# Five landing pads instead of four for the expert weights, and a split of x shared by ScalarE and VectorE

## The reference

```python
x = layer_norm(ALPHA * x + mixer(x))            # conv group and RG-LRU group, w_in, w_out
logits = x @ router_w + router_b                # 32 experts
top_v, top_i = top_k(logits, 4); gate = softmax(top_v)
for e in experts:                               # tokens sorted by expert, no dropping
    g  = minimum(xe @ wg[e] + bg[e], 7)         # (1024 x 1024)
    up = clip(xe @ wu[e] + bu[e], -7, 7)
    ye = ((up + 1) * g * sigmoid(1.702 * g)) @ wd[e] + bd[e]
    out[tokens] += gate * ye
x = layer_norm(ALPHA * x + out)
```

## Time and profile before

| what | us |
|---|---|
| median of three runs | 1111.76 |
| profiled execution | 1111.99 |
| its span | 1110.3 |
| TensorE busy | 1071.7 |
| GpSimd busy | 754.0 |
| VectorE busy | 346.6 |
| ScalarE busy | 201.3 |

### The profile page before, as it was taken

The page is one execution under the profiler, slowest core; times in us unless marked ns, Lnnn a source line. Parts: engine busy times, 40 slices in busy tenths (PEclk is TensorE's granted clock), DMA queues, the critical chain, the costliest instruction groups (busy, mean ns, idle before and its releaser), DMA issues.

```text
span 1110.3 us, 14430 instructions
## 1 busy us (share of the span) xinstructions
PE 1071.7 (97%) x5190; PEld 432.3 (39%) x5191; DVE 346.6 (31%) x593; ACT 201.3 (18%) x331; POOL 754.0 (68%) x778
## 2 busy tenths in 40 slices
PE   8999988999999999999999999999999999999994
PEld 6766343333333333333333333333333333333331
DVE  2638485232232122223222321222212221122214
ACT  1252042111111111111111111111111111111112
POOL 1001117888888478888888888888888888888861
PEclk9999999999999999999999999999999999999998
DMA  9934736999999969999999999999999999999992
GB/s 310 386 119 164 299 119 259 427 429 429 428 429 429 420 269 431 428 429 428 429 429 429 429 429 428 429 428 427 429 429 429 430 428 427 430 427 428 430 425 78
DMA packets 38589, 423.96 MB, mean 382 GB/s; under 512 B 6011, under 2 KB 6011, under 8 KB 13998
## 3 DMA queue, kind: packets, MB, share of 16 engines
q1 hardware_dynamic: 38368, 423.52, 91.3%
q10 hardware_dynamic: 206, 0.24, 0.1%
HBM read 422.32 MB, written 1.42 MB: 382 GB/s over the span
## 4 chain that ended last, share of the span: by engine, by line
PE 47%; DMA 36%; POOL 10%; DVE 4%; issue 1%; ACT 1%; SPq 0%; DVEq 0%; POOLq 0%
PE bank L1260 27%; DMA area<-in_exp_w_up 12%; DMA area<-in_exp_w_gate 12%; DMA area<-in_exp_w_down 11%; POOL ring L426 7%; PE bank L1084 6%; PE bank L1292 4%; POOL ring L427 2%; PE bank L1199 2%; PE bank L1102 2%; PE bank L1062 2%; PE bank L1216 1%; ACT unit_area L620 1%; PE bank L1315 1%; PE bank L1272 1%
## 5 line engine op out<-in xcount | busy, mean ns | idle before, releaser
L426 POOL COPY ring<-area 128x1024 f32<-128x1024 f32 x414 | 418.7, 1051 | 160.0 <-PE bank L1260 48.4
L1260 PE MATMUL bank<-ring,mixT 128*64 128x512 f32 x2112 | 472.4, 594 | 2.0 <-POOL ring L427 2.0
L1260 PEld LDWEIGHTS bank<-ring,mixT 128*64 128x64 f32 x2112 | 149.0, 137 | 298.8 <-issue 287.2
L1260 PE MATMUL bank<-ring,unit_area 128*64 128x512 f32 x1056 | 233.9, 595 | 9.4 <-ACT unit_area L620 9.4
L971 DVE TENSOR_SCALAR bank<-bank 128x512 f32<-128x512 f32 x33 | 23.1, 699 | 529.8 <-PE bank L1260 529.8
L426 POOL COPY ring<-late_pad 128x1024 f32<-128x1024 f32 x135 | 135.5, 1043 | 41.4 <-DMA late_pad<-in_exp_w_up 13.8
L427 POOL COPY ring<-area 128x1024 f32<-128x1024 f32 x138 | 146.0, 1058 | 0.0
L1260 PEld LDWEIGHTS bank<-ring,unit_area 128*64 128x64 f32 x1056 | 75.3, 137 | 145.2 <-issue 144.8
L1292 PE MATMUL bank<-unit_area,area 64*128 64x512 f32 (+1 forms) x396 | 98.8, 615 | 0.8 <-ACT unit_area L625 0.8
L613 ACT ACTIVATE unit_area<-bank 128x512 f32<-128x512 f32 x33 | 19.7, 597 | 299.3 <-DVE bank L971 299.3
L932 DVE TENSOR_SCALAR unit_area<-member,area 128x128 f32<-128x128 bf16 x96 | 64.9, 730 | 20.2 <-PE bank L1315 19.5
(11 more groups left out here) (241 smaller groups left out, 653.7 us busy)
## 6 DMA issues: line engine op xcount, KB each, us to landing
area<-in_exp_w_gate SPq DMA_DIRECT2D x47, 2048.0 KB, 15.2
area<-in_exp_w_up SPq DMA_DIRECT2D x46, 2048.0 KB, 15.2
area<-in_exp_w_down SPq DMA_DIRECT2D x45, 2048.0 KB, 15.2
late_pad<-in_exp_w_up SPq DMA_DIRECT2D x15, 2048.0 KB, 15.2
late_pad<-in_exp_w_gate SPq DMA_DIRECT2D x15, 2048.0 KB, 15.2
late_pad<-in_exp_w_down SPq DMA_DIRECT2D x15, 2048.0 KB, 15.2
ring<-in_w_in SPq DMA_DIRECT2D x4, 2048.0 KB, 12.3
ring<-in_exp_w_down SPq DMA_DIRECT2D x3, 2048.0 KB, 12.0
```

Source lines behind the costliest of these rows:

```text
L426: g.tensor_copy(ring[:, s, c * D:(c + 1) * D], src(s)[:, c * D:(c + 1) * D])
L1260: last = mm(bank[b][side * UT:(side + 1) * UT, :], lhsT, w[:, c, side * HALF:(side + 1) * HALF], start=m == 2 and hf == 0 and c == 0, stop ...
```

## The change

Memory is laid out anew. `area` is now exactly four pads and `late_pad` the fifth. For this the first layer norm's `ln_g` moves into the unused quarter of `late_pad`; the router's and planner's small tiles move out of `area` into `unit_area`; `rms`, `spread`, `place`, `gate_of` and `gates_T` become tensors of their own; `states` lies in `spread`, `states_out` in `mixT`; the down bias and the gated member rows lie in `ln_b`, free after the first layer norm; the second layer norm's vectors lie in pad 3, loaded at the very end.

SyncE loads slots 0 to 3 of expert 1 in the head (slot 3 behind `rmsa_psum`), slot 4 into `late_pad` behind split and seeds. The down bias comes behind the first layer norm. Loads and copies are unrolled over five experts in a loop.

The split is shared: VectorE subtracts, ScalarE casts. GpSimd clears the unused half of a part, and its copies begin when the split is done. ScalarE's seeds and its copies of the gates change places, the transposed gates use bank 3, and TensorE waits for them ahead of the gather, not of the up product.

```diff
+LOOP_END = 27
...
+        ln_g = late_pad[:, 3 * D:4 * D]
...
-        AREA = 15600
+        AREA = 4 * SLOTW
...
-        pads = [area[:, i * SLOTW:(i + 1) * SLOTW] for i in range(3)] + [late_pad[:, :]]
+        rms = sb("rms", [P, 6])[:, :]
+        spread = sb("spread", [P, T])[:, :]
+        states = spread[:, 0:4 * 64].rearrange("p (a b) -> p a b", b=64)
+        pads = [area[:, i * SLOTW:(i + 1) * SLOTW] for i in range(4)] + [late_pad[:, :]]
+        ln2_g, ln2_b = (area[:, 3 * SLOTW + i * D:3 * SLOTW + (i + 1) * D] for i in range(2))
...
+        down_bias = ln_b[:, 0:HALF]
+        gated = ln_b[:, HALF:HALF + 3 * P].rearrange("p (a b) -> p a b", b=P)
+        area, AREA = unit_area, 4 * HALF
...
+        rests = [unit_area[:, 0:D], unit_area[:, D:2 * D]]
...
@@ sync @@
-            for g in range(4):
-                h_ = g % 2
-                sp.dma_start(down_bias[g * NE:(g + 1) * NE, :], a["exp_b_down"][0][:, h_ * HALF:(h_ + 1) * HALF])\
-                    .then_inc(S["down_bias_in"], 16)
+            sp.wait_ge(S["rmsa_psum"], 1)
+            sp.dma_start(pad_of(1, 3), slot_src(3, 1)).then_inc(pad_loaded[3], 16)
             for s, done in ((5, "lru_psum"), (3, "out_psum")):
...
-            for v, name in ((ln_g, "ln2_g"), (ln_b, "ln2_b")):
-                sp.dma_start(v[:, :], a[name].partition_broadcast(P).rearrange("p o n -> p (o n)"))\
-                    .then_inc(S["ln2_in"], 16)
+            for g in range(4):
+                h_ = g % 2
+                sp.dma_start(down_bias[g * NE:(g + 1) * NE, :], a["exp_b_down"][0][:, h_ * HALF:(h_ + 1) * HALF])\
+                    .then_inc(S["down_bias_in"], 16)
             def pad_load(s, e, dst):
 
-                if s < 4:
-                    sp.wait_ge(slot_loaded[s + 2], e * 16 + 16 * PRIOR[s + 2])
+                if s < NSLOT - 1:
+                    sp.wait_ge(slot_loaded[s + 1], e * 16 + 16 * PRIOR[s + 1])
                 else:
-                    sp.wait_ge(slot_loaded[s - 4], e * 16 + 16 * (PRIOR[s - 4] + 1))
+                    sp.wait_ge(slot_loaded[0], e * 16 + 16)
...
             sp.wait_ge(S["seeded"], 6)
             sp.wait_ge(S["parts_ok"], 3)
-            sp.dma_start(pad_of(1, 3), slot_src(3, 1)).then_inc(pad_loaded[3], 16)
-            for s in range(4, NSLOT):
-                pad_load(s, 1, pad_of(1, s))
+            sp.dma_start(pad_of(1, 4), slot_src(4, 1)).then_inc(pad_loaded[4], 16)
+            pad_load(5, 1, pad_of(1, 5))
+            with sp.Fori(2, LOOP_END, len(pads)) as e:
+                for k in range(len(pads)):
+                    for s in range(NSLOT):
+                        pad_load(s, e + k, pad_of(2 + k, s))
...
+            sp.wait_ge(slot_loaded[4], 16 * (NE - 1 + PRIOR[4]))
+            for v, name in ((ln2_g, "ln2_g"), (ln2_b, "ln2_b")):
+                sp.dma_start(v[:, :], a[name].partition_broadcast(P).rearrange("p o n -> p (o n)"))\
+                    .then_inc(S["ln2_in"], 16)
...
@@ gpsimd @@
+            pool.wait_ge(S["out_psum"], 3)
+            pool.wait_ge(x1_ok[0], 1)
+            g.memset(x_parts[7][UT:P, :], 0.0).then_inc(S["low_zero"], 1)
             pool.wait_ge(S["tab_ok"], 1)
+            pool.wait_ge(S["parts_ok"], 3)
+            pool.wait_ge(S["low_zero"], 1)
...
@@ scalar @@
             s_.copy(xTu, bank[3][:, :]).then_inc(S["xu_ok"], 1)
+            for t in range(2):
+                act.wait_ge(S["rest_ok"], t + 1)
+                s_.copy(x_parts[3 * t + 1], rests[t]).then_inc(S["mid_ok"], 1)
+            act.wait_ge(S["rest_ok"], 3)
+            s_.copy(x_parts[7][0:UT, :], rests[0][0:UT]).then_inc(S["mid_ok"], 1)
+            s_.copy(x_parts[6][UT:P, :], rests[0][0:UT]).then_inc(S["mid_ok"], 1)
+
+            act.wait_ge(S["banks_open"], 1)
...
             act.wait_ge(S["gates_T_psum"], 1)
...
@@ vector @@
-            v.memset(x_parts[7][UT:P, :], 0.0).then_inc(S["low_zero"], 1)
+            dve.wait_ge(S["gathered"], 1)
+            dve.wait_ge(S["gated_ok"], 1)
             for t in range(2):
                 dve.wait_ge(S["hi_ok"], t + 1)
-                settle(v.tensor_tensor(rest, x[:, t, :], x_parts[3 * t], ALU.subtract))
-                settle(v.tensor_copy(x_parts[3 * t + 1], rest))
-                settle(v.tensor_tensor(x_parts[3 * t + 2], rest, x_parts[3 * t + 1], ALU.subtract))
-                v.sem_inc(S["parts_ok"], 1)
+                v.tensor_tensor(rests[t], x[:, t, :], x_parts[3 * t], ALU.subtract).then_inc(S["rest_ok"], 1)
+            dve.wait_ge(S["rest_ok"], 2)
+            dve.wait_ge(S["mid_ok"], 1)
+            v.tensor_tensor(x_parts[2], rests[0], x_parts[1], ALU.subtract).then_inc(S["parts_ok"], 1)
+            dve.wait_ge(S["parts_ok"], 1)
             dve.wait_ge(S["hi_ok"], 3)
...
+            v.tensor_tensor(rests[0][0:UT], x[0:UT, 2, :], x_parts[6][0:UT, :], ALU.subtract)\
+                .then_inc(S["rest_ok"], 1)
+            dve.wait_ge(S["states_dma"], 96)
+            dve.wait_ge(S["mid_ok"], 2)
+            v.tensor_tensor(x_parts[5], rests[1], x_parts[4], ALU.subtract).then_inc(S["parts_ok"], 1)
+            dve.wait_ge(S["rest_ok"], 3)
+            dve.wait_ge(S["mid_ok"], 4)
+            v.tensor_tensor(x_parts[7][0:UT, :], rests[0][0:UT], x_parts[7][0:UT, :], ALU.subtract)\
                 .then_inc(S["parts_ok"], 1)
...
@@ tensor @@
-                if results == gates_transposed:
-                    pe.wait_ge(S["gates_T_ok"], 1)
                 biased(1, 1).then_inc(S["gu_bias_used"], 1)
                 product(1, 1, xTu, "up_done", e, pieces=not more_to_come)
                 if more_to_come:
+                    pe.wait_ge(S["gates_T_ok"], 1)
                     pe.wait_ge(S["parts_ok"], 3)
```

More of the change, by code:

```diff
@@ L87, in hybrid_layer @@
         router_b = sb("router_b", [P, NE])
-        ln_g = sb("ln_g", [P, D])
         ln_b = sb("ln_b", [P, D])
@@ L158, in hybrid_layer @@
         first_place = carve(P, 3)
-        assert at[0] <= head_tail
-        at[0] = head_free
         picked = carve(P, 3, TOPK * NE)
-        spread = carve(P, T)
-        unit_area = sb("unit_area", [P, 5 * HALF + P + UT + 3 * P])
-        hTu, hid, sig, y_rows, down_bias = (unit_area[:, i * HALF:(i + 1) * HALF] for i in range(5))
-        rest = unit_area[:, HALF:3 * HALF]
-        gates_T = unit_area[:, 5 * HALF:5 * HALF + P + UT]
-        gated = unit_area[:, 5 * HALF + P + UT:].rearrange("p (a b) -> p a b", b=P)
+        hTu, hid, sig, y_rows = (unit_area[:, i * HALF:(i + 1) * HALF] for i in range(4))
+        rests = [unit_area[:, 0:D], unit_area[:, D:2 * D]]
         xT_flat = xT[:, :, :].rearrange("p c t -> p (c t)")
@@ L311, in _ @@
             sp.wait_ge(S["parts_ok"], 3)
[L312 to L321 removed]
+            sp.dma_start(pad_of(1, 4), slot_src(4, 1)).then_inc(pad_loaded[4], 16)
[4 more added lines that the diff above has]
+                        pad_load(s, e + k, pad_of(2 + k, s))
+            for last in range(LOOP_END, NE - 1):
+                for s in range(NSLOT):
+                    pad_load(s, last, pad_of(last, s))
             for s in range(3):
@@ L429, in _ @@
             move_pads(1, slice(0, 1), lambda s: pad_of(1, s))
-            with pool.Fori(2, NE - 2, 2) as e:
-                move_pads(e, bass.ds(e - 1, 1), lambda s: pad_of(2, s))
-                move_pads(e + 1, bass.ds(e, 1), lambda s: pad_of(3, s))
-            move_pads(NE - 2, slice(NE - 3, NE - 2), lambda s: pad_of(NE - 2, s))
+            with pool.Fori(2, LOOP_END, len(pads)) as e:
+                for k in range(len(pads)):
+                    move_pads(e + k, bass.ds(e + (k - 1), 1), lambda s, k=k: pad_of(2 + k, s))
+            for last in range(LOOP_END, NE - 1):
+                move_pads(last, slice(last - 1, last), lambda s, last=last: pad_of(last, s))
             move_pads(NE - 1, slice(NE - 2, NE - 1), lambda s: pad_of(NE - 1, s), 3)
@@ L593, in _ @@
             s_.copy(xTu, bank[3][:, :]).then_inc(S["xu_ok"], 1)
+            for t in range(2):
[5 more added lines that the diff above has]
+            act.wait_ge(S["banks_open"], 1)
+            for t, (t0, n) in enumerate(TILES):
+                for h_ in range(2):
+                    s_.mul(sum_bank(t, h_), x[0:n, t, h_ * HALF:(h_ + 1) * HALF], ALPHA).then_inc(S["seeded"], 1)
             act.wait_ge(S["gates_T_psum"], 1)
@@ L598, in _ @@
                 if t == 0:
-                    s_.copy(gates_T[rows, P:], bank[1][0:NE, 2 * P:T])
-                last = s_.copy(gates_T[rows, 0:P], bank[1][0:NE, t * P:(t + 1) * P])
+                    s_.copy(gates_T[rows, P:], bank[3][0:NE, 2 * P:T])
+                last = s_.copy(gates_T[rows, 0:P], bank[3][0:NE, t * P:(t + 1) * P])
             last.then_inc(S["gates_T_ok"], 1)
-            act.wait_ge(S["banks_open"], 1)
-            for t, (t0, n) in enumerate(TILES):
-                for h_ in range(2):
-                    s_.mul(sum_bank(t, h_), x[0:n, t, h_ * HALF:(h_ + 1) * HALF], ALPHA).then_inc(S["seeded"], 1)
```

35 lines of the change are left out of this document (11 added, 24 removed).

## The result

The changed kernel takes **1105.7 us** (median of 6 runs, 1103.8 to 1105.99) against 1111.62 before (6 runs beside them, 1109.08 to 1112.63): ratio of the means 0.9948, 95% interval 0.9935 to 0.9961. That is 5.9 us faster in the medians; 8.6 were forecast, and the time lies in the forecast range. A second measurement, further down, shows that these six runs missed a slower outcome that the kernel also has. One later execution of the changed kernel, 1864.64 us at a granted clock of 0.558, is left out of every figure.

A forecast was written before the change was run, and what follows sets the result against it. TensorE, busy 97% of the span, was taken as the bound, with DMA nearly as full. From 1111.99 us, 5.72 (split) and 3.0 (fifth pad) came off, giving 1103.3; the forecast was 1103.2, range 1100.8 to 1107.8.

The forecast's parts named there:

- The split ends at 169.0, not 175.8: In the head, sharing the split of x between VectorE and ScalarE was to finish it at 169.0 us instead of 175.8.
- Members 172.7, gates 172.6, sigmoid 174.5: Around unit 0's up product: forecast end times in us of VectorE's member rows, ScalarE's gate copies and its sigmoid.
- Gain 5.72 between up and down product: In unit 0, the down product was to start 10.77 us behind the up product instead of 16.49, gaining 5.72 us.
- what VectorE's split of x costs: The prediction's single cause for unit 0's extra 5.72 us between up and down product, compared with unit 7.
- The down product at 178.4; wrong if behind 180: Unit 0's down product was to start at 178.4 us; a start behind 180 would show the forecast wrong.
- Fifth pad 3.0, with 1.9 in hand: Behind the double unit, one more pad puts DMA 4.90 us ahead, removing 3.0 us of late data with 1.9 spare.
- DMA sets the whole end: Rival: DMA bounds the kernel to the end, so the pad pays its full 4.90 us: 1101.4 us, chance 0.12.
- Longer empty stretch of DMA before 386: A sign of the forecast: DMA, further ahead, would stand empty for longer before 386 us; no size given.
- The fourth load in the head does no harm and little good: Loading a fourth slot of expert 1 in the head delays expert 0's slots 4.9 us, harmlessly; DMA has room there.
- GpSimd's copies begin behind the split: cover 10 us, cost nothing: GpSimd's copies start at 169.0 instead of 163.68 us; the first is still ready about 10 us before unit 1.
- member rows beside copies, 2.39 us, already hidden: Argument against the rival of a slower kernel (1116.5 us, chance 0.07): VectorE's member rows beside GpSimd's copies cost no time.
- The second layer norm's loads: At the end, these loads follow the last expert's slots, landing by 1082.5 us, 4.5 us before VectorE's statistics at 1087.0.

The follow-up runs named there:

- e5: Changed kernel with the whole split back on VectorE and GpSimd's copies not waiting for it; five pads and new layout kept: 1108.0 us.
- e3: Changed kernel with GpSimd's copies begun early, not waiting for the shared split: 1103.51 us.
- e1: Changed kernel with four pads instead of five and only slots 0 to 2 of expert 1 loaded in the head: 1107.2 us.
- e7: Changed kernel with slot 3 of expert 1 loaded behind the split instead of in the head, five pads kept: 1103.34 us.
- e9: Changed kernel with hidden rows transposed ahead of gated member rows and slot 3 of expert 1 loaded behind the split: 1100.15 us.
- e2: Changed kernel with the whole split on VectorE as before, GpSimd's copies still begun behind it: 1114.59 us.
- e6: Changed kernel with hidden rows transposed, and copied by ScalarE, ahead of the gated member rows: 1101.39 us.
- e8: Changed kernel with hidden rows transposed first and GpSimd's copies begun early, not waiting for the split: 1100.9 us.
- e11: Changed kernel with GpSimd's first copy held further, until unit 0's first hidden rows are there: 1121.61 us.
- e10: Changed kernel with three dummy matmuls ahead of unit 0 and slot 3 of expert 1 loaded behind the split: 1103.64 us.
- after_again: The changed kernel itself, unedited, measured again over 11 executions: median 1103.48 us, seven at 1102.68 to 1105.42 and four at 1111.34 to 1114.06.
- e4: Changed kernel with three dummy matmuls in TensorE's two short gaps just ahead of unit 0: 1112.85 us.

## Why the prediction was right, and where not

- **The split ends at 169.0, not 175.8.** Right: 168.86. ScalarE's cast beside VectorE is 1.04 to 1.09 us, not 0.99; the sum hardly feels it.
- **Members 172.7, gates 172.6, sigmoid 174.5.** Right: 172.97, 172.14, 174.05. The hidden rows came at 178.20, not 176.6, but TensorE was 2.06 us late by then: from the start of the up product it is 8.51 us, and 8.97 were worked out. The sum had left out that the second clamp waits for the end of the up product; it cost nothing.
- **Gain 5.72 between up and down product.** Right in size: 5.80. But "what VectorE's split of x costs" is too much for one cause: the split proper is 3.2 (e5 against e3), 1.2 is the memset and what moved with it, and 1.4 is the lower clock behind the gap.
- **The down product at 178.4; wrong if behind 180.** It started at 180.38, and by the letter this test failed. All 2.06 us of it lie ahead of the up product (169.69 instead of 167.63), which the prediction held fixed: 0.43 of head and 1.63 of lower clock. The place between the products is as forecast. The clock is this prediction's mis-sized term: it counted as gained that the low stretch behind the earlier trace rows's gap goes, and didn't ask whether one would come elsewhere. It came. Among profiles of kernels with the same gaps ahead of unit 0, e1, e7, e9 and the first profile have it at unit 0 (first half 4.99 to 5.30 us); before, e2, e3, e5, e6, e8, e11 and the second profile of the same kernel (3.60) haven't, and of these e3 and e5 (like e10) pay it in unit 32. What decides is not settled.
- **Fifth pad 3.0, with 1.9 in hand.** Right: 3.06 by e1, no wait for GpSimd left. "DMA sets the whole end" (1101.4) falls with it: it would have paid 4.90. The Trainium skill's rule that HBM, and not SBUF, is almost always the end-to-end bottleneck ("SBUF — State Buffer", "A bandwidth-pool intuition that's wrong (but worth ruling out)") does not hold for this kernel, whose chain is 93% TensorE; in e8 and e9, with units of 27.77 us, it starts to bite in the last three units.
- **Longer empty stretch of DMA before 386.** Wrong in its place, right in kind: DMA still moves from 382 to 386 (share 0.33) and moves nothing from 386 to 390; GpSimd's idle time grew from 16.46 to 22.65 us (its copy at 387.75). (A slip beside it: DMA begins 175.8 - 171.1 = 4.7 us earlier, not 4.8.)
- **The fourth load in the head does no harm and little good.** No good, as e7 shows (916.3 both). The harm was missed, next point.
- **"GpSimd's copies begin behind the split: cover 10 us, cost nothing."** This step failed. It asked if each slot is there in time for TensorE, and it is. It did not ask what a late start does to the copies that follow: with four slots landed, ten slots are copied without a pause, past the moment when VectorE's member rows for unit 1 are due, and these wait for the run's end. In 4 of the 17 runs of the changed kernel the gain was gone (1111.34 to 1114.06); the one of them that was profiled shows this cause. Nor is "member rows beside copies, 2.39 us, already hidden" a bound: that row is of a stretch in which VectorE got in between.
- **The second layer norm's loads.** Forecast 1082.5 for the last; issued at 1061.08 and 19.6 us to landing: 1080.7. Statistics began at 1089.09. Covered.

Why the median still hit the range: the six runs of the result are all below 1106, and in the profiled one the member rows were not held; that is luck, since 4 of the next 11 were above 1111. Against that the head was late in the profiled one (160.10, where the second profile has 158.33), and what clock and head took against before (2.06 profiled) is most of the difference between 8.6 and 5.9.

## What to carry to other kernels

When a helper engine's start is moved back while its inputs pile up, don't check only its first delivery: lay out the whole run until its first forced pause, and look at which other engine's instructions that run can hold out. A one-line test for such a joint is the longest single duration of a cheap instruction, not its mean: in after_again the 96 member instructions have 0.30 us at least, 1.07 in the middle and 12.7 at most. Compare profiles stretch by stretch, from the opening of a unit, and not by their ends alone: here the head moved them by up to 5 us. And run a kernel with timing this close often enough to see both outcomes; six runs did not.

## What the runs showed of the hardware

- One VectorE instruction, bf16<-f32 of 128x64 (0.30 us when free), waited for a whole run of GpSimd copies: 12.6 us (e4), 12.7 (the changed kernel), 12.9 (e6), 14.5 (e2), 20.5 (e11), always ending within 0.1 us of the last copy's end. In other stretches the same three instructions took 2.2 to 3.0 us in all beside equally dense copies, none of them over 1.18, about one copy. One thing sets the five apart: they began 18.9 to 26.8 us into an unbroken run of copies. Of the others in all fourteen profiles, those right behind a held one aside, none began later than 13.9 us into one (in the first profile unit 1's began 0.5 us into one, behind the gap at 197.80). So a long unbroken run goes with the hold in every profile. Whether its age is the cause, and where the limit lies, no run shows: the first profile's gap closed 0.48 us before the member rows began, so VectorE did not simply slip into it. The f32 clamp just ahead of it (0.70 us, in and out of a bank) was not held.
- The Trainium skill, "SBUF — State Buffer", "🔬 SBUF: two separate sides", calls the pair of ports that VectorE and GpSimd share an exclusive lock: a GpSimd instruction, or a VectorE one in a 2-port mode or with two inputs in SBUF (against a GpSimd one that reads SBUF), holds it for the whole instruction if it starts first, and the other blocks. No row names the mode of the member instructions. The rows agree that VectorE blocks; one GpSimd copy takes 1.04 us, and the wait was 12 to 20 of them long, which this rule alone does not give.
- VectorE's subtraction (two f32 inputs) beside copies took 2.05 us instead of 1.22, and the copies 1.66 each (4.99 for three) instead of 1.00: there both were slowed.
- TensorE gaps of 0.42 and 0.68 us ahead of unit 0 were followed by a granted clock of 0.50 in some executions and of 1.00 in others of the same kernel; filled with matmuls (e4, e10) it was 1.00 in both profiles.
